# Reordered waits and idle-time multiplications in a two-block fp32 transformer kernel on TensorE

## The reference

```python
def first_block(x, mem, ...):
    # layer a: differential attention, 6 heads of two maps, and memory attention, 4 heads
    proj = rms_norm(x, a_norm) @ a_w_in                      # q, k, v, qm, gate
    q, k = apply_partial_rope(rms_norm(q)), apply_partial_rope(rms_norm(k))
    o  = rms_norm(diff_attention(q, k, v, lam), a_subln) * (1 - lambda_init)
    om = memory_attention(qm, mem, ...)                      # rms_norm of mem and of heads
    x  = x + (concat(o, om) * silu(gate)) @ a_w_out
    # layer b: stick breaking attention with its own keys and values, memory attention again
    k_s, v_s = split(rms_norm(x, kv_norm) @ w_kv_shared)
    proj = rms_norm(x, b_norm) @ b_w_in                      # q, qm, gate
    x  = x + (concat(stick_breaking_attention(q, k_s, v_s), memory_attention(...)) * silu(gate)) @ b_w_out

def second_block(x, ...):
    for l in range(2):
        h = rmsnorm(x, pre_norm_g[l])
        u, v, z_a, c_q, c_kv, k_rope, z_b, x_c, z_c, g_a, g_b, g_c = split(h @ w_in[l])
        y_a = gmlp_spatial(u, v, ...) * silu(z_a)
        y_b = mla_attention(c_q, c_kv, k_rope, ...) * silu(z_b)      # 8 heads
        y_c = rg_lru(x_c, ...) * silu(z_c)                           # 1280 channels
        merged = sum(sigmoid(g) * (y @ w_proj) for the three branches)
        x = x + rmsnorm(merged @ w_out[l], post_norm_g[l])
```

## Time and profile before

| what | value |
|---|---|
| median of 3 runs | 2351.34 us (2350.88 to 2352.33) |
| the profiled execution's time | 2353.74 us |
| its span | 2351.9 us |
| instructions | 27364 |
| busy share: TensorE, its weight loads, DVE, ACT, GpSimd | 94%, 72%, 50%, 39%, 49% |
| read from device memory | 187.56 MB, 81 GB/s over the span |

### The profile page before, as it was taken

One profiled execution on the slowest core, in us unless ns is written; L12 is line 12 of the kernel. 1 busy time (PEld: TensorE's weight loads), 2 busy tenths in 40 slices (PEclk: granted clock), 3 DMA queues, 4 the chain that ended last, 5 costly groups with the idle time before them and its releaser, 6 DMA issues.

```text
span 2351.9 us, 27364 instructions
## 1 busy us (share of the span) xinstructions
PE 2219.3 (94%) x9986; PEld 1694.2 (72%) x9986; DVE 1174.4 (50%) x1821; ACT 927.7 (39%) x1573; POOL 1143.0 (49%) x1360
## 2 busy tenths in 40 slices
PE   6899899999899999999999999799999999999996
PEld 4676567765577667888887788576678888877785
DVE  6777775448645342043238744463420342198443
ACT  4546643345424453232223632344432322237322
POOL 3553236642246324565456675363144665575751
PEclk9999999999999999999999999899999999999998
DMA  3222112321122113323233232222133232332321
GB/s 141 72 85 68 37 64 91 106 63 37 37 81 90 54 36 112 103 90 99 81 99 92 75 111 90 63 81 63 37 100 97 90 99 83 97 99 72 117 81 63
DMA packets 53124, 191.42 MB, mean 81 GB/s; under 512 B 6016, under 2 KB 6400, under 8 KB 52480
## 3 DMA queue, kind: packets, MB, share of 16 engines
q1 hardware_dynamic: 51696, 184.44, 25.2%
q10 hardware_dynamic: 1296, 5.24, 0.6%
HBM read 187.56 MB, written 2.10 MB: 81 GB/s over the span
## 4 chain that ended last, share of the span: by engine, by line
PE 82%; DVE 9%; ACT 4%; issue 2%; POOL 2%; DMA 1%; DVEq 0%; SPq 0%; ACTq 0%
PE proj L539 20%; PE proj L541 20%; PE proj L540 20%; PE score L535 5%; PE proj L535 4%; PE turned L535 2%; PE mix L535 2%; PE stat L535 2%; POOL lower L491 2%; PE score L540 1%; PE score L539 1%; PE score L541 1%; PE ptp L771 1%; DVE small L1657 1%; DMA raw_ring<-stream 1%
## 5 line engine op out<-in xcount | busy, mean ns | idle before, releaser
L491 POOL TENSOR_TENSOR lower<-raw_ring,upper 128x256 fp32r<-128x256 f32 x1340 | 1125.2, 873 | 1151.2 <-ACT upper L1128 1150.9
L539 PE MATMUL proj<-h,upper 128*128 128x512 f32 x1440 | 587.3, 408 | 9.4 <-issue 3.6
L1128 ACT ACTIVATE upper<-raw_ring 128x1024 fp32r<-128x1024 f32 x335 | 350.9, 1058 | 563.4 <-PE proj L539 319.2
L541 PE MATMUL proj<-h,lower 128*128 128x512 f32 x1440 | 565.1, 392 | 0.0
L540 PE MATMUL proj<-h,upper 128*128 128x512 f32 x1440 | 564.4, 392 | 0.0
L539 PEld LDWEIGHTS proj<-h,upper 128*128 128x128 f32 x1440 | 272.8, 189 | 70.2 <-issue 10.7
L541 PEld LDWEIGHTS proj<-h,lower 128*128 128x128 f32 x1440 | 272.2, 189 | 58.6
L540 PEld LDWEIGHTS proj<-h,upper 128*128 128x128 f32 x1440 | 272.8, 189 | 54.7 <-issue 4.3
L539 PE MATMUL proj<-y,upper 128*128 128x512 f32 x600 | 243.5, 406 | 10.1 <-ACT yf L1216 3.5
L541 PE MATMUL proj<-y,lower 128*128 128x512 f32 x600 | 238.6, 398 | 0.0
L540 PE MATMUL proj<-y,upper 128*128 128x512 f32 x600 | 238.4, 397 | 0.0
(11 more groups left out here) (401 smaller groups left out, 3376.9 us busy)
## 6 DMA issues: line engine op xcount, KB each, us to landing
raw_ring<-stream SPq DMA_DIRECT2D x335, 512.0 KB, 3.5
landing<-stream SPq DMA_DIRECT2D x5, 512.0 KB, 9.7
x<-x_in SPq DMA_DIRECT2D x4, 512.0 KB, 6.5
rows<-rows_in ACTq DMA_DIRECT2D x2, 1024.0 KB, 5.2
out<-x SPq DMA_DIRECT2D x8, 256.0 KB, 2.0
memraw<-mem_in SPq DMA_DIRECT2D x1, 1024.0 KB, 13.0
memraw<-mem_in ACTq DMA_DIRECT2D x1, 1024.0 KB, 4.8
rot<-tables_in ACTq DMA_DIRECT2D x2, 512.0 KB, 3.3
```

What stands on the lines that cost most here:

```text
L491: ins = nc.gpsimd.tensor_tensor(lower[:, p % RING, a:b], slot_source(p)[:, a:b], upper[:, p % RING, a:b].bitcast(FP32), ALU.subtract)
L539: first_ = nc.tensor.matmul(o, lhsT[0], rhs[0], start=start, stop=False)
L541: return first_, nc.tensor.matmul(o, lhsT[1], rhs[0], start=False, stop=stop)
L1128: nc.scalar.activation(upper[:, p % RING, :], slot_source(p), ACT.Copy).then_inc(split_upper, 1)
```

## The change

The change keeps the arithmetic and the streamed weights and reorders work on TensorE, ACT and DVE. It does this:

- `spin(n)` multiplies the 128 columns of the matrix of ones by itself n times into bank mix: 6 times at the start, 16 times after the sum of x's squares, 12 times at each layer's start, and 12 times before the squares at the end of layer 0 of the second block.
- Heads of a: the squares of mem are summed in two halves between the head sums, into bank mix, and its root is computed at the end by ACT and four operations of DVE.
- The values of mem for layer a are made at the beginning of the attention loop (`begin`), into other banks. For layer b they are made between the head sums of the memory keys (`between`), and ACT feeds no slots while these keys are taken.
- The keys of b start with `behind` 1; the takes of v1 in b feed the ring after each group; b.q0 stands between the head sums, and the last query tile goes into the beginning of the attention.
- Attention: the root is split over two steps (`root_begun`, `root_ended`), differential tiles end one step later, the second memory tile mixes into stat, two gate units remain for after the loop, and the SiLUs follow the attention.
- Layers: zb0 stands before the latent sum of cq, the second pair of heads is projected at the beginning of the MLA attention into ptp, proj[0], mix and stat, maxima are taken two instead of three steps ahead, and the wait for the last mixed tile stands behind `out_and_merge`.
- At the very end five of the eight tiles of x are added on TensorE: the identity times x, then the identity times the scaled tile, into one bank each; ACT copies the sums to x.

```diff
+SUMMED = 5
...
+    def sum_bank(d):
+        return (score + [ptp, mix, turned])[d][:, :]
...
-    def mix_of(kind, e):
-        return stat if kind == "mla" and e else mix
+    def mix_of(kind, t, e):
+        return stat if kind == "mla" and e or kind == "mem" and t else mix
...
-        steps = {"diff": 4 * MT, "mem": 16}[kind]
-        return min(8 * gates_of(kind) * (z + 1) // steps, 8 * gates_of(kind))
+        if kind == "diff":
+            return 2 * (z + 1)
+        return min(z + 1, 14)
...
+        def spin(n):
+            for _ in range(n):
+                mm(mix[:, 0:P], c("ones"), c("ones"), True, True)
...
             if together:
                 together()
+                pe.wait_ge(late_consts, 16 * N_LATE)
                 summed()
+                memory_squares(0, KT // 2)
                 summed()
+                memory_squares(KT // 2, KT)
+                summed()
+                rotated(0)
                 jobs[4]()
-                rotated(0)
                 summed()
-                summed()
+                rotated(1)
                 jobs[5]()
-                rotated(1)
                 rotated(2)
                 summed()
...
+                if i == len(jobs) and between:
+                    between()
                 if i:
                     summed()
...
+        spin(6)
         m = C.next("norm")
...
+        spin(16)
...
-                group(S, C, W, names("b.k", 4), h, hkey)
+                group(S, C, W, names("b.k", 4), h, hkey, 1)
...
-                heads(S, C, W, [lambda n=n: full(S, C, W, n, h, hkey) for n in names("b.qm", 2)], 0)
-                for n in names("b.q", MT):
+                heads(S, C, W, [lambda n=n: full(S, C, W, n, h, hkey) for n in names("b.qm", 2)], 0,
+                      between=lambda: full(S, C, W, "b.q0", h, hkey))
+                for n in names("b.q", MT - 1)[1:]:
                     full(S, C, W, n, h, hkey)
...
+            def memory_values():
+                tokens(S, C, W, names("mem0.v", 2), mh, None, MEM, 2, places=(0, 5))
+                pe.wait_ge(*S.after("vm", 0, 1))
+                pe.wait_ge(*S.after("heads_ready", "m0"))
...
+            for _ in range(2):
+                next(gates)
...
+            spin(12)
             group(S, C, W, names("ckv", KVR) + names("cq", QR)[:2], h, hkey)
             full(S, C, W, "cq2", h, hkey)
             latent_sum("ckv", KVR, raw[:, 1, :])
             full(S, C, W, "kr", h, None)
+            full(S, C, W, "zb0", h, None)
             latent_sum("cq", QR, raw[:, 0, :])
-            full(S, C, W, "zb0", h, None)
...
+            def second_pair():
+                up(22, QR, 0, place=4)
+                up(22 + QR, QR, 0, at=0)
+                up(28, KVR, QR, place=5)
+                up(28 + KVR, KVR, QR, place=7)
+                pe.wait_ge(*S.after("read", last_at[4]))
...
-            pe.wait_ge(*S.after("mix_used", C.n["tile"] - 1))
...
             out_and_merge("b", KT)
+            pe.wait_ge(*S.after("mix_used", C.n["tile"] - 1))
...
             if l < LAYERS - 1:
+                spin(12)
                 squares(S, C, c("ones"), KT)
+                continue
...
+            for d in range(SUMMED):
+                mm(sum_bank(d), c("ident"), x[:, d, :], True, False)
+            for d in range(SUMMED):
+                pe.wait_ge(*S.after("scaled", d))
+                mm(sum_bank(d), c("ident"), mixed[:, d, :], False, True).then_inc(*S.mark("added_x", ("x_sum", d)))
...
-                    j, k, t = next_job(S, C), C.next("head"), C.next("sq")
+                    j, k, t = next_job(S, C, between is not None and cols == MEM), C.next("head"), C.next("sq")
...
-                memory(1)
+                heads(S, C, 2, MEM, between=lambda: (feed(wanted[0]), memory_values(1, None)))
...
-                    take(S, C, v1[:, b, a:z], cols=z - a, keys_=[("values_ready", s)], block=b)
+                    take(S, C, v1[:, b, a:z], cols=z - a, keys_=[("values_ready", s)], block=b, later=s == "b")
+                feed(wanted[0])
...
-                    ahead += [(maxima, 3 if kind == "mla" else 2, kind), (weights, 1, kind)]
-            run(kinds, ahead, now, [(lambda kind, t: finish[kind](t, at.tile[kind] + t), {"diff": 3, "mla": 2}.get(kind, 1), kind)
+                    ahead += [(maxima, 2, kind), (weights, 1, kind)]
+            run(kinds, ahead, now, [(lambda kind, t: finish[kind](t, at.tile[kind] + t), {"diff": 4, "mla": 2}.get(kind, 1), kind)
...
+            for d in range(SUMMED):
+                act.wait_ge(*S.after("x_sum", d))
+                nc.scalar.activation(x[:, d, :], sum_bank(d), ACT.Copy).then_inc(*S.mark("taken", ("x", d)))
...
-                link(S, scaled(mixed[:, d, :], mixed[:, d, :], lc(l, "post", d), sd))
+                link(S, scaled(mixed[:, d, :], mixed[:, d, :], lc(l, "post", d), sd), ("scaled", d))
+                if l == LAYERS - 1 and d < SUMMED:
+                    continue
```

More of the change, by code:

```diff
@@ L369, in lead, with run @@
         return 3
-    def run(kinds, ahead, now, after):
+    def run(kinds, ahead, now, after, begin=None):
         steps = [step for kind in kinds for step in steps_of(kind)]
         for z in range(-max(d for _, d, _ in ahead), len(steps) + max(d for _, d, _ in after)):
+            if z == 0 and begin:
+                begin()
             for f, d, kind in ahead:
@@ L591, in full, with tokens @@
                 W.finish(name)
-        def tokens(S, C, W, slots, src, key, width, blocks, first_tile=0, reads=False):
+        def tokens(S, C, W, slots, src, key, width, blocks, first_tile=0, reads=False, places=None):
             j0 = C.n["job"]
@@ L790, in mixing @@
                 pe.wait_ge(*S.after("pt", s))
-                if tile:
+                if kind == "mem" and t:
+                    pe.wait_ge(*S.after("sums_used", C.n["norm"] - 1))
+                elif tile:
                     pe.wait_ge(*S.after("mix_used", tile - 1))
@@ L1222, in take_gate, with attention @@
                  waits=[("gate_used", g - 2)] if g >= 2 else [])
-        def attention(S, C, kinds, after=(), gates=None, ends=lambda left: None):
-            scores4, ptps = beside if gates else apart
+        def attention(S, C, kinds, after=(), gates=None, begin=None):
+            scores4, ptps = beside
             at = Bases(C, kinds)
-            last = at.end["step"] - 1
             def prob(kind, s, m):
@@ L1326, in act_program @@
                 nc.scalar.activation(small[:, 10:12], ptp[:, 0:2], ACT.Exp).then_inc(*S.mark("lam_exps", ("lam_exps",)))
-                memory(0)
-            else:
-                heads(S, C, 2)
-                for t in range(MT):
+                heads(S, C, 2, MEM)
+                act.wait_ge(*S.after("heads_ready", "m0"))
+            else:
+                heads(S, C, 2, between=lambda: take(S, C, q1[:, 0, :], keys_=[("qk_ready", s)]))
+                for t in range(1, MT - 1):
                     take(S, C, q1[:, t, :], keys_=[("qk_ready", s)])
```

179 lines of the change are left out of this document (107 added, 72 removed).

## The result

The changed kernel takes 2328.61 us in the median of four runs (2325.97 to 2329.05), beside 2351.11 for the kernel before in the same comparison: a ratio of 0.9903 with a 95% interval of 0.9885 to 0.992. It is 22.5 us faster. Forecast were 33.6, a time of 2317.7 and a range of 2304 to 2335, so the direction and the range held, and the gain was two thirds of what the sum said.

What follows compares the result with a forecast made beforehand. TensorE, busy 94% of the span, was taken as the bound, with time to gain only in its idle gaps and half clock stretches. The parts' terms summed to -33.6 us, a median of 2317.7, range 2304 to 2335.

Steps and rivals of the forecast that it cites:

- D: Differential attention: root split over two steps removes 0.77 us gaps, and some half clock goes; -7.7 us, bounds -3 and -10.
- E: Memory layer 1 and first keys of b: later feeds delay GpSimd's remainders; a loss of 4.4 us, bounds -3 and +7.
- L: 12 spins at each layer's start: gain limited by when DVE's h is ready; -2.0 us, bounds 0 and -5.8.
- H: zb0 ahead of the latent sum covers TensorE's wait for DVE's half_var; -5.5 us over both layers, bounds -3 and -6.
- F: Rest of b's inputs: gaps at v1's takes and those covered by b.q0 and b.q5 go; -6.3 us, bounds -2 and -8.
- C: Memory values moved into the beginning of attention a: first transposed block comes later; a loss of 2.0 us, bounds 0 and +3.5.
- B: Heads of attention a: split memory squares fill waits, memory root leaves the chain; -8.0 us, bounds -5.5 and -9.
- G: Memory part and end of b: DVE paces, two gate units left for the end; -1.0 us, bounds +1 and -4.
- K: Wait for the mixing bank moved behind out_and_merge: a 1.61 us wait goes in each layer; -3.2 us, bounds -2 and -4.
- halved: Rival, chance 0.22: DVE and ACT soon give the next limit, B, D, F and H bring half; -17.2 us, 2334.
- slower: Rival, chance 0.04: the ring of weights starves where feeds are deferred, 11.8 us a place; with four places 2360.5 us.
- A: Start of the kernel: spins fill waits before the first products, which DVE's h ends; 0 us, bounds -1 and +1.

Runs made afterwards that it cites:

- experiment 1: Changed kernel with the takes of v1 in layer b feeding the ring before each take again, as in the kernel before: 2323.33 us, ratio 0.9883.
- experiment 3: Changed kernel with both feed deferrals undone, at v1's takes and at layer b's memory keys: 2317.91 us, ratio 0.9855 to the kernel before.
- experiment 4: Changed kernel with the values of mem for layer a computed ahead of the attention's loop again: 2326.67 us, ratio 0.989 to the kernel before.

## Why the prediction was right, and which steps failed

The direction and the range were right, because the gaps of the list were real and most of them closed. By the table, D, E, M and each row of L, H and I came within 0.4 us of their terms. D, H and M were also undone on the chip (3.6 to 4.4 for D's root alone, 4.6 to 5.4 and 3.1 to 3.9).

The size was right only in part, and by some luck. Against their terms F lost 7.4, C 2.4, B 1.5 and G 1.2 us; K gave 5.1 more than its term, for a reason that the prediction did not have, and the other rows 1.6 more. That leaves 5.9 between 33.6 and the 27.7 of the spans, and the step from spans to medians adds 5.2. Without K's surplus the time would be nearly that of the rival "halved". It is not that rival's case, though: of B, D, F and H only F brought less than half.

**F** is the step that failed: it said -6.3 and gave +1.1. "The gap of 1.71 at 428.66 goes, as v1's takes no longer stand behind feeds of slots" was read from one side only. The takes no longer waited for the feeds, and the feeds now waited for the takes. GpSimd idled 15.93 us and TensorE then 5.86. This is the mechanism of the "slower" rival, which named v1's takes as a place, with a price of 11.8 each. The rival was dismissed because GpSimd was "ahead of TensorE" there; it was ahead only because ACT fed it early. One such place came true, at 5.3 us by experiment 1; without it F is -5.1, near its term. The second half of F, b.q0 and b.q5, gave 3.0 of 4.6 here, behind products that the 5.86 had put at half clock.

**E** had the right number and the right engine. It said that the deferred feeds cost, and experiment 3 gives 5.4 for them. Its sign read otherwise than forecast: the row names ACT's take of vm, which stood behind the waiting feed, and not GpSimd's lower. The good bound, "the value jobs fill the gap", did not come about: TensorE is done with them when the 9.38 begins at 364.97.

**C** was +4.4 and not +2.0. The chain through exps was right. But behind the wait of 3.83 the scores and the first 15 of the 48 products of the values ran at half clock (0.41 an entry until 187.3, then 0.28), and the sum had no half clock in this part. With the values ahead of the loop (experiment 4) the part is +1.0.

**B** gave -6.5 where -8.0 stood: a gap of 3.69 stayed in front of the third head sum, where 3.2 idle and 0.5 of the chain had been kept, and half clock followed it, which the sum had taken to be gone. The clock over 48.30:73.40 is 0.93, by which I estimate 3.5 us at half clock, worth up to 1.8.

**G** expected -1.0 and gave +0.2. With the gates of the last steps kept for later, TensorE waits 1.45, 0.31, 0.56 and 0.47 between 621 and 626, and the last mixing behind these waits takes 3.68 us (626.04), where the kernel before took 1.94 (635.80). That the held back gates are the cause was not tried.

**K** gave -8.3 in two layers instead of -3.2. The two waits of 1.61 are gone. The other 5 lie inside the MLA attention, where 0.73 in front of a transposition and, in layer 1, a stretch at half clock from 1662 disappeared. The maxima taken one step later may have done this, or the other banks and place of the second pair; neither was tried alone.

**L** was sized at 2.0 by DVE's h. The traces show the products at full clock and the 1.26 wait for h in layer 1. The medians show 0.2, or nothing. The term counted on full clock behind both spins; its bound of 0 named the other case, and that one came in layer 0 in one execution of the changed kernel and in layer 1 in the other.

The Trainium skill's rule (TensorE: Matmul & The Clock Gate, HAM oscillation: throttled time costs half its length) would have given 6.8 for this part, and that is not what the runs show: where the clock stayed at 0.50, there was nothing to give back, and where it was full, DVE's h was next due. As a price of TensorE's own time the rule is not refuted; as a price of the kernel's time it leaves out who comes next.

The spins of **A** were sized by a misread row. The 16 entries of 3.61 us in the earlier trace rows are 8 multiplications of two entries each, and so are the "16 multiplications for the squares of mem" of the kernel's description. One of 256 columns takes 0.45, and one of 128 columns about 0.23, twice the estimate. It cost nothing, as the first product waits for DVE's h either way: 23.06 us with them, 23.52 before.

Last, "I take the same distance after" was wrong: 2.6 us one way before and 2.6 the other after. The time of one profiled execution is the median give or take the half clock stretches that it happened to have.

## What to carry to other kernels

Where one engine both feeds a ring and clears results in program order, a deferral of the feed is paid by whoever stands behind the ring: look at the idle time of the engine that follows the feed (5.27, 10.20 and 15.93 us here), not only at the releaser of the gap. Undoing two such deferrals was worth 5.3 and 5.4 us, together nearly half of what the whole change had brought.

When two kernels are compared by one profile each, look first at which stretches ran at the lower clock in each: here the same program gave spans 5.2 us apart.

## What the runs showed of the hardware

- Whether a stretch behind a gap runs at half clock is not settled by the program and the gap. In two executions of the changed kernel the gap in front of layer 0 (2.56 and 2.55 us) was followed by half clock in the first and by full clock in the second, and the gap of 1.91 us in front of layer 1 by full clock in the first (1.00 in 1509.00:1513.30) and by 0.50 from 1513.7 to 1517.1 in the second.
- A spin is dearer than I had estimated: 12 of them are 24 entries and take 2.84 us at full clock, 0.24 each and not 0.11.

```profile
1504.26 2.84 PE L543 MATMUL mix<-const 128*128 128x128 f32 x24
```

- GpSimd's remainder of a slot takes 2.8 us when DVE is idle (the row below, of experiment 1, in which DVE does nothing from 453.40 to 456.30) and mostly 3.9 to 4.1 when DVE works beside it: in the windows view of 364.20 to 377.60 DVE is busy 12.91 of 13.40 us, and GpSimd's two slots at 361.10 take 8.29. So a place at which DVE is full is also one at which the ring of weights is slow.

```profile
453.42 2.83 POOL L499 TENSOR_TENSOR lower<-raw_ring,upper 128x256 fp32r<-128x256 f32 x4 [3.71 <-ACT upper L1188]
```
